# Expert outputs: a table in DRAM that is gathered and added at the end, against accumulating scatters into the residual in DRAM, block by block

## The chip, the cores and the metric

One core of one Trainium2 chip runs the kernel. The metric is the device time of one launch in microseconds (us). TensorE (PE) multiplies and transposes, VectorE (DVE) and ScalarE (ACT) do elementwise work and bring results out of PSUM, GpSimd (POOL) does elementwise work and issues the indirect DMAs, SyncE (SP) issues the weight loads. All DMAs of all queues run on the core's 16 DMA engines.

## The reference

A decoder of two layers over 1024 tokens of width 1024, in float32. Each layer has an attention and pooling half, and then a mixture of experts on which the change acts:

```
x = x + concat(att, pool) @ w_out
h = rms_norm(x)
g = top-1 of 4 groups; (e1, e2) = top-2 of the group's 4 experts        # 16 experts
w1, w2 = softmax over (e1, e2) * p_group                                # the gates
a = silu(h @ w_gate[e]) * (h @ w_up[e]) * gate[e]                        # 256 wide
x = x + sum over e of a[e] @ w_down[e]
```

The output is x after two layers.

## The kernel before

**Stages of a layer.** An input stage (`in_pe`, `in_act`, `in_dve`) turns x into q, k, v, u tile by tile: 8 tiles of 128 tokens, first for q and v, then for k and u, with every product split in three. Attention follows, then the output projection (`out_pe`, `out_act`, `out_dve`), which adds into the residual `xr` (8 tiles, 128 x 1024, in SBUF for the whole kernel), norms it, stores the normed rows in the DRAM tensor `token_rows`, and computes the router's logits. DVE then computes, in one chain of small instructions, where each of the 2048 (token, expert) rows goes: rows are sorted by expert into blocks of 128, at most 31 blocks (`BLOCKS`). Two 16-step matmuls of one-hot matrices (`in_row`, `in_block`) turn the positions into a list of tokens for each block, `row_tok`. How many blocks are used depends on the data; `used` is loaded into a register of each engine. This run uses 22 in the first layer and 23 in the second.

**The expert stage.** In the slot of block t, PE runs `gate_up(t)` (16 matmuls by the profile, line 1521), `xtm(t+1)` (transposes of the next block's rows), `down(t-1)` (8 matmuls, line 1534) and the transposes of `act`. ACT runs the Silu of t, then `moe_down(t-1)`: it copies the upper half of the block's result into `y[slot]`, waits until DVE has copied the lower half, and issues the store of the 512 KB block into the DRAM tensor `y_table` (line 809). Only then it copies `aT(t)`, which PE's `down(t)` reads. `xg` and `y` have three buffers each (`RING`). POOL gathers the rows of block j (`load_rows`, line 578) as soon as the transposes of block j-3 are done. For unused blocks POOL gathers too (all their indices are token 0), while PE, ACT and DVE skip them and only raise their semaphores. SP loads the three weight tensors of an expert, 1 MB each, into four slots as experts end.

**The end of a layer.** When all gathers and stores have been issued and landed, POOL gathers for each tile t and each of its two choices k the rows of `y_table` by `pos_i` (line 594, 16 gathers of 512 KB, four pairs of buffers), and DVE adds them with their gates into `xr` (lines 1261 and 1263), one tile after the other; in the first layer the norms and splits of the next layer's first tiles stand between the additions. ACT's second step of the next input stage waits for `x_ready` of all 8 tiles, and so does SP's load of the third part of `w_in`. After the second layer POOL writes `xr` to `out_x` tile by tile (line 600).

Of the kernel before, what the change touches and what calls it, by code (L numbers as in the profile page):

```python
# [63 lines left out]
C_ALL = C_INV + 16  # L64
# [8 lines left out]
GATHS = 4  # L73
SLOTS = 4
BIAS = BLOCKS


def shape_constants():
# [19 lines left out]
    c[:, C_TOK:C_TOK + 2 * T] = np.tile(P * np.arange(T), 2)[None, :] + row  # L98
# [4 lines left out]
    c[:, C_INV:C_INV + 16] = 1.0 / (1.0 + np.arange(16))  # L103
    return c


def trunk(nc, x, norm1_gain, w_in, q_norm_gain, k_norm_gain, w_pool, pool_scale, w_out,
# [7 lines left out]
    with ctx:  # L115
# [8 lines left out]
        y_table = nc.dram_tensor("y_table", (ROWS, D), f32, kind="Internal").ap()  # L124
# [32 lines left out]
        pos_i = sb("pos_i", [P, 2, T], i32)  # L157
        row_tok = sb("row_tok", [P, 32], i32)
        next_tok = sb("next_tok", [P, RING], i32)
# [10 lines left out]
        u_flat = big[:, AT_U:AT_U + K * 512]  # L170
        raw_in = [W[:, 1, :, :], W[:, 3, :, :], kT_r.rearrange("p (k n) -> p k n", k=K),
# [17 lines left out]
        gath = [big[:, AT_K + 2 * D * i:AT_K + 2 * D * (i + 1)].rearrange("p (k n) -> p k n", k=2) for i in range(GATHS)]  # L189
# [29 lines left out]
        in_block = A[:, 5120:5376].bitcast(f16).rearrange("p (c b) -> p c b", b=32)  # L219
        junk2 = A[:, 6144:6656].bitcast(bf16)  # L220
# [69 lines left out]
        routed = sem("routed")  # L290
        w_loaded = sem("w_loaded")
# [17 lines left out]


# [5 lines left out]
        s_wpool, s_fill = sem("s_wpool"), sem("s_fill")  # L316
# [3 lines left out]
        s_y = [sem(f"s_y{i}") for i in range(RING)]  # L320
        s_gath = [sem(f"s_gath{i}") for i in range(GATHS)]
        s_out = sem("s_out")
# [62 lines left out]
        for name, n in (("lg", T * NR), ("ge", T * EG), ("ee", T * EG), ("gm", T), ("gs", T), ("pt", T),  # L385
                        ("is1", T * 4), ("sm", T), ("goh", T * EG), ("es", T * EPG), ("m1", T), ("oh1", T * 4),
                        ("es2", T * EPG), ("m2", T), ("oh2", T * 4), ("dm", T), ("e2", T), ("rd", T),
                        ("te", NE), ("start", NE), ("cnt", NE), ("posf", 2 * T), ("blk", 2 * T), ("bef", 32), ("M", T * NE)):
# [21 lines left out]
        def _(sp):  # L410
# [16 lines left out]
            with sp.Fori(0, DEPTH) as l:  # L427
# [8 lines left out]
                    .then_inc(s_wpool, 16)  # L436
                sp.wait_ge(rows_t, 1)
# [47 lines left out]
        def _(pool):  # L485
# [24 lines left out]
            for j in range(2 * SEQ // P, BLOCKS):  # L510
                pool.dma_start(y_table[j * P:(j + 1) * P, :], xr[:, 0, :]).then_inc(s_fill, 16)
            with pool.Fori(0, DEPTH) as l:
# [58 lines left out]
                def load_rows(j, slot, m):  # L571
                    if not first(j):
# [4 lines left out]
                    ch.link(nc.gpsimd.tensor_copy(next_tok[:, slot:slot + 1], row_tok[:, ds(j, 1)]))  # L577
                    pool.indirect_dma_start(
                        out=xg[slot], out_offset=None, in_=token_rows,
                        in_offset=bass.IndirectOffsetOnAxis(ap=next_tok[:, slot:slot + 1], axis=0)).then_inc(s_xg[slot], 16)  # L580

                ch.restart()
                steps(pool, BLOCKS, load_rows, ch, ring=RING)


                for i in range(RING):
                    pool.wait_ge(s_y[i], (l + 1) * (16 * USES[i]) + 1)
                    pool.sem_inc(s_passed, 1)
                for t in range(T):
                    if t >= GATHS:  # L590
                        pool.wait_ge(x_ready, upto(l + 1, T, t - GATHS + 1))
                        pool.sem_inc(s_passed, 1)
                    for k in range(2):
                        pool.indirect_dma_start(
                            out=gath[t % GATHS][:, k, :], out_offset=None,
                            in_=y_table, in_offset=bass.IndirectOffsetOnAxis(ap=pos_i[:, k, t:t + 1], axis=0),
                        ).then_inc(s_gath[t % GATHS], 16)
            for t in range(T):
                pool.wait_ge(x_ready, upto(DEPTH, T, t + 1))
                pool.dma_start(out[0, t * P:(t + 1) * P, :], xr[:, t, :]).then_inc(s_out, 16)  # L600
            pool.wait_ge(s_out, 16 * T)


        @block.scalar
        def _(a_):
# [4 lines left out]
            for s in s_y + s_tok:  # L610
                a_.sem_inc(s, 1)
# [37 lines left out]
            with a_.Fori(0, DEPTH) as l:  # L649
# [28 lines left out]
                def in_act(t, par_, h):  # L678
# [917 lines left out]
```

## Time and profile before

| | us |
|---|---|
| median of 3 runs (lowest, highest) | 1797.02 (1796.76, 1799.8) |
| profiled execution, its own time | 1796.23 |
| span of its trace | 1794.2 |
| PE busy in the span | 1496.5 |
| DVE, ACT, POOL busy | 831.2, 485.1, 272.3 |

The span is what the profiler's records cover; the profiled execution took 2.03 us more than it. Busy time of PE includes matmuls that stand in its pipeline. Places in the trace: the expert stage of the first layer lies at 580 to 852 us, that of the second at 1455 to 1740 us.

### The profile page before, as it was taken

What the parts mean: (1) busy time and instruction counts of PE and PEld (TensorE: products, weight loads), DVE (VectorE), ACT (ScalarE), POOL (GpSimd) and SP (SyncE); (2) the same over time, 40 slices, a digit from 0 to 9 for tenths busy, and PEclk for the clock granted to TensorE, in tenths of its full rate; (3) what the DMA queues carried; (4) which work ended last, traced back from release to release, by engine and by line L of the source; (5) the groups of instructions that cost most, each with busy time, mean ns of one, the idle gap of its engine ahead of it and who ended that gap; (6) DMA issues with size and microseconds to landing.
All of it is one profiled execution on the core that took longest, in us unless ns stands there. A gap on an engine that the chain in (4) does not pass through costs nothing.

```text
span 1794.2 us, 23296 instructions
## 1 busy us (share of the span) xinstructions
PE 1496.5 (83%) x6931; PEld 1073.7 (60%) x6932; DVE 831.2 (46%) x2101; ACT 485.1 (27%) x916; POOL 272.3 (15%) x259
## 2 busy tenths in 40 slices
PE   3999977888993999998269998888899749999960
PEld 2887866777882444444158786777768624444430
DVE  3777666565436122211377766665543442222114
ACT  3222156663211011111212212566611201111000
POOL 1200058002001011110300001920200021111114
PEclk8999989999996999999589999899999869999985
DMA  8400020000047588942640002000000845888637
GB/s 302 164 29 0 0 95 1 0 0 0 36 147 263 163 294 299 368 158 88 245 161 0 1 0 94 1 0 0 0 12 35 295 138 172 296 301 293 225 123 287
DMA packets 118473, 228.11 MB, mean 127 GB/s; under 512 B 6184, under 2 KB 72816, under 8 KB 118416
## 3 DMA queue, kind: packets, MB, share of 16 engines
q1 hardware_dynamic: 90352, 129.55, 21.1%
q0 software_dynamic: 18128, 65.71, 10.3%
q10 hardware_dynamic: 9936, 32.14, 4.4%
q8 instruction: 30, 0.49, 0.1%
q14 instruction: 27, 0.22, 0.0%
HBM read 183.33 MB, written 44.04 MB: 127 GB/s over the span
## 4 chain that ended last, share of the span: by engine, by line
PE 71%; DVE 10%; issue 8%; ACT 5%; DMA 4%; ACTq 1%; POOL 0%; DVEq 0%; PEld 0%; POOLq 0%; SPq 0%; PEldq 0%
PE ps L1521 18%; PE ps L1315 17%; PE ps L1448 9%; PE ps L1295 9%; PE ps L1534 8%; PE ps L1408 5%; ACT arena L730 2%; PE ps L1462 2%; DMA arena<-token_rows,next_tok 1%; ACT arena L742 1%; DMA big<-y_table,pos_i 1%; DVE arena L1021 1%; DVE w_in_lo L913 1%; PE ps L1375 1%; PE ps L1377 1%
## 5 line engine op out<-in xcount | busy, mean ns | idle before, releaser
L1295 PE MATMUL ps<-cst,arena 128*128 128x128 f32 x1682 | 247.7, 283 | 145.4 <-DVE arena L884 56.9
L1521 PE MATMUL ps<-big,arena 128*128 x720 | 325.3, 605 | 10.6 <-issue 9.9
L1295 PEld LDWEIGHTS ps<-cst,arena 128*128 128x128 f32 x1682 | 199.1, 145 | 223.2 <-DVE arena L884 59.1
L874 DVE TENSOR_TENSOR arena<-ps,par 128x512 f32<-128x512 f32 x126 | 81.2, 687 | 365.2 <-PE ps L1295 365.2
L1521 PEld LDWEIGHTS ps<-big,arena 128*128 128x128 f32 x720 | 135.5, 193 | 171.5 <-issue 171.5
L1315 PE MATMUL ps<-w_in_hi,hT_hi 128*128 128x512 f32 x512 | 206.8, 404 | 12.6 <-DVE w_in_lo L913 8.6
L1315 PE MATMUL ps<-w_in_lo,hT_hi 128*128 128x512 f32 x512 | 202.2, 395 | 0.0
L1315 PE MATMUL ps<-w_in_hi,hT_lo 128*128 128x512 f32 x512 | 202.2, 395 | 0.0
L1534 PE MATMUL ps<-big,arena 128*128 x360 | 166.6, 607 | 7.0 <-issue 7.0
L1408 PE MATMUL ps<-big,arena 128*128 x1152 | 149.6, 276 | 0.0
L1408 PEld LDWEIGHTS ps<-big,arena 128*128 128x128 f32 x1152 | 144.7, 193 | 5.4
L577 POOL COPY next_tok<-row_tok 128x1 int32 (+1 forms) x62 | 14.9, 240 | 781.7 <-PE ps L1295 450.7
L1021 DVE CUSTOM_DVE_ANT_0 arena<-ps,cst 128x128 f32<-128x128 f32 (+7 forms) x128 | 96.7, 756 | 69.4 <-PE ps L1377 68.4
L730 ACT ACTIVATE arena<-arena,st 128x128 f32<-128x128 f32 (+7 forms) x128 | 99.2, 775 | 79.0 <-DVE st L1021 76.9
L1315 PEld LDWEIGHTS ps<-w_in_hi,hT_hi 128*128 128x128 f32 x512 | 98.3, 192 | 35.3 <-DVE w_in_lo L913 10.4
L1534 PEld LDWEIGHTS ps<-big,arena 128*128 128x128 f32 x360 | 66.6, 195 | 74.8 <-issue 74.8
L1315 PEld LDWEIGHTS ps<-w_in_hi,hT_lo 128*128 128x128 f32 x512 | 97.9, 191 | 21.3
L1315 PEld LDWEIGHTS ps<-w_in_lo,hT_hi 128*128 128x128 f32 x512 | 98.3, 192 | 19.5
L1448 PE MATMUL ps<-w_o_hi,cat_hi 128*128 128x512 f32 x256 | 103.4, 404 | 7.3 <-DVE cat_lo L1081 7.3
L1448 PE MATMUL ps<-w_o_hi,cat_lo 128*128 128x512 f32 x256 | 100.8, 394 | 0.0
L1448 PE MATMUL ps<-w_o_lo,cat_hi 128*128 128x512 f32 x256 | 100.8, 394 | 0.0
L1375 PE MATMUL ps<-k_high,q_parts 128*128 128x512 f32 (+1 forms) x192 | 82.1, 429 | 11.8 <-DVE k_low L996 11.8
(159 smaller groups left out, 1764.4 us busy)
## 6 DMA issues: line engine op xcount, KB each, us to landing
big<-in_w_gate SPq DMA_DIRECT2D x32, 1024.0 KB, 8.5
big<-in_w_up SPq DMA_DIRECT2D x32, 1024.0 KB, 11.2
big<-in_w_down SPq DMA_DIRECT2D x32, 1024.0 KB, 13.0
y_table<-arena ACTq DMA_DIRECT2D x45, 512.0 KB, 7.0
big<-in_w_in SPq DMA_DIRECT2D x18, 1024.0 KB, 10.6
big<-in_w_out SPq DMA_DIRECT2D x4, 2048.0 KB, 10.2
token_rows<-arena ACTq DMA_DIRECT2D x16, 512.0 KB, 2.8
y_table<-x_res POOLq DMA_DIRECT2D x15, 512.0 KB, 9.5
```

The costliest lines, as they stand in the source:

```text
L730: sc.activation(pr[b][:, 0:nk], pr[b][:, 0:nk], ACT.Exp, scale=-1.0, bias=st[:, 64 + n:65 + n], accum_out=st[:, 80 + n:81 + n]).then_inc(p ...
L742: sc.activation(prT[b][:, 0:nb, :], ps[:, 4, 0:nb * P] .rearrange("p (a c) -> p a c", c=P), ACT.Copy).then_inc(pt0_ev, 1)
L874: ins = ve.tensor_tensor(out=dst[:, 4 * h:4 * h + 4, :], in0=ps[:, banks + h, :].rearrange("p (a c) -> p a c", c=P), in1=spread(gain[:, 4 ...
L1021: ve.tensor_tensor_reduce(out=pr[b][:, 0:nk], in0=ps[:, 2 * b:2 * b + 2, :].rearrange("p a c -> p (a c)")[:, 0:nk], in1=cst[:, C_MASK + SE ...
L1295: ins = te.transpose(ps[:, bank + i // 4, (i % 4) * P:(i % 4 + 1) * P], src, ident)
L1315: ins = te.matmul(ps[:, 2 + 2 * par_ + i, :], a[par_][:, k, :], b[:, k, :], start=k == 0 and n == 0, stop=k == K - 1 and n == 2)
L1375: te.matmul(ps[:, 2 * b + c // 512, 0:w], q_parts[a][:, i * P:(i + 1) * P], k_high[a][:, c:c + w], start=True, stop=False)
L1408: ins = te.matmul(ps[:, 6 + b, 0:P], prT[b][:, j, :], v[:, j, ds(p * P, P)], start=j == 0, stop=j == i)
L1448: ins = te.matmul(ps[:, 2 * par_ + h, :], a[par_][:, k, :], b[:, k, :], start=k == 0 and n == 0, stop=k == K - 1 and n == 2)
L1462: ins = te.matmul(ps[:, 6 + par_, 0:P], h2T[par_][:, k, :], wr_all[:, ds(l * (K * NR) + k * NR, P)], start=k == 0, stop=k == K - 1)
L1521: ins = te.matmul(ps[:, 2, :], xgT[:, k, :], big[:, ds(at + k * 2 * FE, 2 * FE)], start=k == 0, stop=k == K - 1)
L1534: ins = te.matmul(ps[:, 4 + h, :], aT[:, k, :], big[:, ds(at + (E_GU + k * D + 512 * h), 512)], start=k == 0, stop=k == 1)
```

## The change

The kernel's output tensor becomes the residual in DRAM for the expert stage, with 31 x 128 spare rows behind its 1024. In the output projection ACT writes each tile of `xr` to it. The gates are not applied at the end but in the activation: for each block a column of 128 gates (`list_gate`) is made, by cutting the 32 bits of a gate into three integers (11, 11 and 10 bits), sending them through 16 more matmuls of the one-hot matrices, and putting them together. `y[slot]` is then added to the rows `row_dst` of the output by a scatter with `compute_op=add`, issued by POOL. Entries of a block that hold no row, and the whole of unused blocks, go to spare rows. Two scatters may name the same token, so ACT raises `y_whole` for block t only when the scatters of all blocks before t have landed (`s_add`); unused blocks don't wait for that. All 31 scatters are issued in each layer. At the start of the second layer SP waits for all 31 scatters of the first and reads the 8 tiles of `xr` back; after the second layer POOL waits for the last scatter, and the first 1024 rows are the result. `y_table`, its 15 filling stores at the start, `pos_i`, `next_tok`, the 32 gathers and the 32 additions at the layers' ends, and the 8 final stores are gone.

```diff
+C_SPARE = C_INV + 16          # SEQ + 1 + 128*block + row: the spare row of each entry
+AHEAD = 5
+OUT_ROWS = SEQ + ROWS
 # SP, at the start of layer l
+                with sp.If(l > 0):
+                    sp.wait_ge(s_add, upto_added(l, 0))
+                    for t in range(T):
+                        sp.dma_start(xr[:, t, :], out[t * P:(t + 1) * P, :]).then_inc(s_again[t], 16)
+                    for t in range(T):
+                        sp.wait_ge(s_again[t], l * 16)
+                        sp.sem_inc(x_ready, 1)
 # POOL
-            for j in range(2 * SEQ // P, BLOCKS):
-                pool.dma_start(y_table[j * P:(j + 1) * P, :], xr[:, 0, :]).then_inc(s_fill, 16)
-                    ch.link(nc.gpsimd.tensor_copy(next_tok[:, slot:slot + 1], row_tok[:, ds(j, 1)]))
-                steps(pool, BLOCKS, load_rows, ch, ring=RING)
-                for t in range(T):
-                    if t >= GATHS:
-                        pool.wait_ge(x_ready, upto(l + 1, T, t - GATHS + 1))
-                    for k in range(2):
-                        pool.indirect_dma_start(
-                            out=gath[t % GATHS][:, k, :], out_offset=None,
-                            in_=y_table, in_offset=bass.IndirectOffsetOnAxis(ap=pos_i[:, k, t:t + 1], axis=0),
-                        ).then_inc(s_gath[t % GATHS], 16)
-            for t in range(T):
-                pool.wait_ge(x_ready, upto(DEPTH, T, t + 1))
-                pool.dma_start(out[0, t * P:(t + 1) * P, :], xr[:, t, :]).then_inc(s_out, 16)
+                def add_rows(j):
+                    pool.wait_ge(y_whole, upto(l, BLOCKS, j + 1))
+                    pool.indirect_dma_start(
+                        out=out, out_offset=bass.IndirectOffsetOnAxis(ap=row_dst[:, j:j + 1], axis=0),
+                        in_=y[j % RING], in_offset=None, compute_op=ALU.add).then_inc(s_add, 16)
+                for j in range(BLOCKS):
+                    load_rows(j, j % RING, j // RING)
+                    if j == 0:
+                        pool.wait_ge(s_base, (l + 1) * (16 * T))
+                    if j >= AHEAD:
+                        add_rows(j - AHEAD)
+                for j in range(BLOCKS - AHEAD, BLOCKS):
+                    add_rows(j)
+            pool.wait_ge(s_add, upto_added(DEPTH, 0))
 # ACT
-                        if h == 0:
-                            a_.wait_ge(x_ready, upto(l, T, T))
                     a_.dma_start(token_rows[ds(t * P, P), :], xs2[par_]).then_inc(s_tok[par_], 16)
+                    a_.dma_start(out[ds(t * P, P), :], xr[:, t, :]).then_inc(s_base, 16)
@@ moe_down
-                    a_.wait_ge(s_y[slot], l * (16 * USES[slot]) + 16 * m + 1)
+                    a_.wait_ge(y_whole, upto(l, BLOCKS, t + 2 - RING))
                     sc.activation(y[slot][:, 512:1024], ps[:, 5, :], ACT.Copy).then_inc(y1_ready, 1)
                     a_.wait_ge(y0_ready, upto(l, BLOCKS, t + 1))
                     a_.wait_ge(y1_ready, upto(l, BLOCKS, t + 1))
-                    a_.dma_start(y_table[ds(t * P, P), :], y[slot]).then_inc(s_y[slot], 16)
+                    if not first(t):
+                        a_.wait_ge(s_add, upto_added(l, t))
+                    a_.sem_inc(y_whole, 1)
 # DVE, after block_e: dve.wait_ge(s_base, ...), three bit cuts, a cast, a compare, three
 # products into in_gate, three small ones for row_dst; after rows_evac(0) three more that
 # put list_gate together; in_low(l + 1, 0) moves behind them
-                ch.link(ve.tensor_copy(pos_i[:, :, :].rearrange("p k t -> p (k t)"), R("posf")))
-                    ve.tensor_tensor(out=act, in0=ps[:, 2, FE:2 * FE], in1=sg, op=ALU.mult).then_inc(a_ready, 1)
+                    ve.scalar_tensor_tensor(out=act, in0=ps[:, 2, FE:2 * FE], scalar=list_gate[:, ds(t, 1)], in1=sg,
+                                            op0=ALU.mult, op1=ALU.mult).then_inc(a_ready, 1)
-                for t in range(T):
-                    dve.wait_ge(s_gath[b], l * (16 * 2 * (T // GATHS)) + 32 * (t // GATHS + 1))
-                    ch.link(ve.scalar_tensor_tensor(out=xr[:, t, :], in0=gath[b][:, 0, :], scalar=gate_w[:, 0, t:t + 1],
-                                                    in1=xr[:, t, :], op0=ALU.mult, op1=ALU.add))
-                    ve.scalar_tensor_tensor(out=xr[:, t, :], in0=gath[b][:, 1, :], scalar=gate_w[:, 1, t:t + 1],
-                                                in1=xr[:, t, :], op0=ALU.mult, op1=ALU.add).then_inc(x_ready, 1)
 # PE, after xtm(0)
+                pe.wait_ge(gate_parts, upto(l, 1, 1))
+                for c in range(2 * T):
+                    ins = te.matmul(ps[:, 7, 0:96], in_row[:, c, :], in_gate[:, c, :, :].rearrange("p k b -> p (k b)"),
+                                    start=c == 0, stop=c == 2 * T - 1)
```

On POOL, the end of the block loop and of the layer, before. `arena<-token_rows` is a gather of a block's rows, `big<-y_table` a gather for the final additions; the names in brackets are semaphores that are waited for.

```order
L577 COPY next_tok<-row_tok 128x1 [waits s_xg0]
L578 DMA arena<-token_rows,next_tok 128x1024 [waits s_pool]
L587 ISA
L587 ISA [waits s_y0]
L594 DMA big<-y_table,pos_i 128x1024 [waits s_y1,s_y2]
L594 DMA big<-y_table,pos_i 128x1024 x7
L591 ISA
L594 DMA big<-y_table,pos_i 128x1024 [waits x_ready]
```

The same place after the change, where `out_x<-arena,x_res` is a scatter that adds:

```order
L594 DMA arena<-token_rows,row_tok 128x1024 [waits xtm_done,s_xg2]
L602 DMA out_x<-arena,x_res 4992x1024 [waits y_whole]
L590 REGISTER_ALU
L591 REGISTER_ALU [waits xtm_done]
L594 DMA arena<-token_rows,row_tok 128x1024 [waits s_xg0]
L602 DMA out_x<-arena,x_res 4992x1024 [waits y_whole] x3
L600 REGISTER_ALU
L602 DMA out_x<-arena,x_res 4992x1024 [waits y_whole]
```

The scatter of block j-5 stands behind the gather of block j, and the last five stand at the end, where the 16 gathers stood.

On ACT, one slot of the expert stage, before (`L813` is the Silu, `L806` the copy of a block's upper half, `L817` the copy of `aT`):

```order
L812 ISA
L813 ACTIVATE arena<-ps 128x256 [waits gu_done]
L805 ISA [waits dn_done]
L806 ACTIVATE arena<-ps 128x512 [waits s_y1]
L809 ISA [waits y1_ready,y0_ready]
L809 DMA y_table<-arena 128x1024
L817 ACTIVATE arena<-ps 128x256 [waits a_t_done]
```

and after the change:

```order
L827 ISA
L828 ACTIVATE arena<-ps 128x256 [waits gu_done]
L818 ISA [waits dn_done]
L819 ACTIVATE arena<-ps 128x512 [waits y_whole]
L823 ISA [waits y1_ready,y0_ready]
L832 ACTIVATE arena<-ps 128x256 [waits s_add,a_t_done]
```

The store has left ACT's queue, and the wait for the scatters before this block stands in its place, ahead of the copy of `aT`.

## Rows read from the trace of the kernel before

**Rows 1.** The page, part 1: busy time and share of the span.

```profile
PE 1496.5 (83%) x6931; PEld 1073.7 (60%) x6932; DVE 831.2 (46%) x2101; ACT 485.1 (27%) x916; POOL 272.3 (15%) x259
```

**Rows 2.** Windows: stretch, length, each engine's busy us, clock, DMA share, GB/s.

```profile
609.00:768.00 159.00, 158.88 (x474) 77.19 (x473) 30.75 (x53) 19.13 (x42) 15.18 (x27) 1.00 0.88 310
```

**Rows 3.** Timeline: start, length, engine, line; first layer's expert stage on POOL.

```profile
607.60 0.18 POOL L577 COPY next_tok<-row_tok 128x1 int32 x1 [11.35 <-PE ps L1295]
...
839.55 0.18 POOL L577 COPY next_tok<-row_tok 128x1 int32 x1 [10.07 <-PE ps L1295]
```

**Rows 4.** Issue to landing of the block gathers, line 578, 590 to 843 us.

```profile
DMA to landing us min/median/max: 4.3/6.0/7.2
```

**Rows 5.** Issue to landing of the table stores, line 809, 590 to 843 us.

```profile
L809 ACTq DMA_DIRECT2D y_table<-arena x20: 337/339/356, 611.8 to 831.9; - x20
DMA to landing us min/median/max: 2.6/7.2/8.9
```

**Rows 6.** Timeline: one slot, and the next slot's down matmuls.

```profile
612.25 0.38 ACT L817 ACTIVATE arena<-ps 128x256 f32<-128x256 f32 x1 [0.71 <-DVE arena L1220]
...
618.55 3.60 PE L1534 MATMUL ps<-big,arena 128*128 x8
```

**Rows 7.** Timeline and chain of waits: the end of the first layer.

```profile
852.58 0.18 POOL L577 COPY next_tok<-row_tok 128x1 int32 x1 [11.39 <-PEq L1572]
...
866.21 0.97 POOL L578 DMA_INDIRECT arena<-token_rows,next_tok  x1 [0.50 <-POOL next_tok L577]
867.48 0.94 POOL L594 DMA_INDIRECT big<-y_table,pos_i  x1 [0.30 <-issue]
...
877.64 1.06 ACT L624 ACTIVATE arena<-x_res 128x1024 f32<-128x1024 f32 x1 [16.53 <-DVE x_res L1263]
881.18 1.97 PE L1295 MATMUL ps<-cst,arena 128*128 128x128 f32 x8 [29.46 <-DVE arena L884]
```

**Rows 8.** Timeline, last row chain of waits: PE in the second layer's first tiles.

```profile
886.81 0.79 PE L1315 MATMUL ps<-w_in_hi,hT_hi 128*128 128x512 f32 x1 [3.66 <-DVE hT_lo L902]
...
894.49 0.39 PE L1315 MATMUL ps<-w_in_hi,hT_lo 128*128 128x512 f32 x1
...
926.19 1.97 PE L1295 MATMUL ps<-cst,arena 128*128 128x128 f32 x8 [8.39 <-DVE arena L884]
...
928.16 11.54 PE ps L1315 x48
```

**Rows 9.** DMA, 843 to 881 us in 40 slices of 0.95 us, and issues.

```profile
GB/s 203 181 375 0 0 0 0 0 0 0 47 229 358 285 280 399 412 410 423 392 397 395 338 350 330 187 233 267 129 246 323 354 375 397 397 392 414 418 414 418
big<-in_w_in SPq DMA_DIRECT2D x2, 1024.0 KB, 10.0
```

**Rows 10.** Timeline and windows: the end of the second layer.

```profile
1740.14 0.18 POOL L577 COPY next_tok<-row_tok 128x1 int32 x1 [12.78 <-PEq L1572]
1778.36 0.53 POOL L600 DMA_DIRECT2D out_x<-x_res  x1 [2.93 <-DVE x_res L1263]
1740.00:1785.00 45.00, 0.00 (x0) 0.00 (x0) 20.34 (x17) 0.00 (x0) 24.68 (x32) 0.52 0.91 339
1785.00:1794.20 9.20, 0.00 (x0) 0.00 (x0) 0.00 (x0) 0.00 (x0) 0.00 (x0) 0.50 0.00 0
```

**Rows 11.** Page part 6: the read of one tile of x, alone in its queue.

```profile
x_res<-in_x SPq DMA_DIRECT2D x1, 512.0 KB, 3.5
```

**Rows 12.** Timeline: tables and the first block of the first layer.

```profile
567.67 0.69 DVE L1116 TENSOR_TENSOR arena<-arena,cst 128x512 f32<-128x512 f32 x1
572.27 0.40 PE L1498 MATMUL ps<-arena 128*128 128x32 f16 x8 [10.76 <-DVE arena L1194]
575.78 0.18 DVE L1207 TENSOR_SCALAR block_e<-arena 128x32 int32<-128x32 f32 x1
581.92 1.29 DVE L874 TENSOR_TENSOR arena<-ps,par 128x512 f32<-128x512 f32 x2 [0.30 <-PE ps L1295]
584.46 8.87 PE L1521 MATMUL ps<-big,arena 128*128 x16 [2.57 <-issue]
```

More of the change, by code:

```diff
@@ L72 @@
 RING = 3
-GATHS = 4
 SLOTS = 4
+AHEAD = 5
+OUT_ROWS = SEQ + ROWS
 BIAS = BLOCKS
@@ L97, in shape_constants @@
     c[:, C_JJ:C_JJ + P] = np.arange(P)
-    c[:, C_TOK:C_TOK + 2 * T] = np.tile(P * np.arange(T), 2)[None, :] + row
+    c[:, C_TOK:C_TOK + 2 * T] = np.tile(P * np.arange(T), 2)[None, :] + row + 1
     c[:, C_DESC:C_DESC + 4] = 4 - np.arange(4)
@@ L103, in shape_constants @@
     c[:, C_INV:C_INV + 16] = 1.0 / (1.0 + np.arange(16))
+    c[:, C_SPARE:C_SPARE + 32] = SEQ + 1 + P * np.minimum(np.arange(32), BLOCKS - 1)[None, :] + row
     return c
@@ L188, in trunk @@
                 for i in range(SLOTS)]
-        gath = [big[:, AT_K + 2 * D * i:AT_K + 2 * D * (i + 1)].rearrange("p (k n) -> p k n", k=2) for i in range(GATHS)]
         def ring(at, size, n=2, inner=None):
@@ L290, in trunk @@
         routed = sem("routed")
+        gate_parts = sem("gate_parts")
+        gates_listed = sem("gates_listed")
+        y_whole = sem("y_whole")
         w_loaded = sem("w_loaded")
@@ L319, in trunk @@
         s_xg = [sem(f"s_xg{i}") for i in range(RING)]
-        s_y = [sem(f"s_y{i}") for i in range(RING)]
-        s_gath = [sem(f"s_gath{i}") for i in range(GATHS)]
-        s_out = sem("s_out")
+        s_base, s_add = sem("s_base"), sem("s_add")
+        s_again = [sem(f"s_again{t}") for t in range(T)]
         s_ms = sem("s_ms")
@@ L607, in _ @@
             for s in (params, q_high_in, k_high_in, win_top, gain_in, sd1, sqz_done, sdz, cat_top, v_copied, u_copied, t_evac, p_ready, pt0_ev, at_ev, sd2,
-                      ge_exp, dm_exp, silu_done, aT_ready, y1_ready):
+                      ge_exp, dm_exp, silu_done, aT_ready, y1_ready, y_whole):
                 a_.sem_inc(s, BIAS)
-            for s in s_y + s_tok:
+            for s in s_tok:
                 a_.sem_inc(s, 1)
@@ L825, in maybe_down @@
                         a_.sem_inc(y1_ready, 1)
-                        a_.sem_inc(s_y[slot], 16)
+                        a_.sem_inc(y_whole, 1)
                 def maybe_act(t, slot, m):
@@ L1197, in _ @@
                 dve.wait_ge(listed, upto(l, 1, 1))
-                ve.tensor_copy(row_tok[:, :], ps[:, 2, 0:32]).then_inc(rows_known, 1)
+                ve.tensor_scalar(row_tok[:, :], ps[:, 2, 0:32], -1.0, 0.0, ALU.add, ALU.max).then_inc(rows_known, 1)
                 ch.link(ve.tensor_copy(start_i[:, 0:NE], R("start")))
@@ L1209, in _ @@
                 dve.sem_inc(s_passed, 1)
+                dve.wait_ge(s_base, (l + 1) * (16 * T))
+                dve.sem_inc(s_passed, 1)
+                bits = gate_w[:, :, :].rearrange("p k t -> p (k t)").bitcast(i32)
+                ve.tensor_scalar(gate_bits[:, 0, :], bits, 0x7FF, None, ALU.bitwise_and)
+                ve.tensor_scalar(gate_bits[:, 1, :], bits, 11, 0x7FF, ALU.logical_shift_right, ALU.bitwise_and)
+                ch.link(ve.tensor_scalar(gate_bits[:, 2, :], bits, 22, None, ALU.logical_shift_right))
+                ch.link(ve.tensor_copy(R("parts"), gate_bits[:, :, :].rearrange("p k c -> p (k c)")))
+                parts = R("parts").rearrange("p (k c) -> p k c", k=3)
+                tt(R("tmp3", 32), spread(R("blk"), 32), count, ALU.is_equal)
+                for k in range(3):
+                    ins = ve.tensor_tensor(out=in_gate[:, :, k, :], in0=R("tmp3", 32), in1=spread(parts[:, k, :], 32),
+                                           op=ALU.mult)
+                ins.then_inc(gate_parts, 1)
+                ch.link(ve.tensor_scalar(R("spare"), ps[:, 2, 0:32], 0.0, None, ALU.is_equal))
+                tt(R("spare"), R("spare"), cst[:, C_SPARE:C_SPARE + 32], ALU.mult)
+                ch.link(ve.scalar_tensor_tensor(out=row_dst[:, :], in0=ps[:, 2, 0:32], scalar=-1.0, in1=R("spare"),
+                                                op0=ALU.add, op1=ALU.add))
                 used = dve.value_load(start_i[0:1, NE:NE + 1], min_val=2 * SEQ // P, max_val=BLOCKS)
```

69 lines of the change are left out of this document (35 added, 34 removed).

## The prediction

> **What bounds the kernel now.** I read the page first: PE is busy for 83% of the span, every other engine for less than half [rows 1]. So a change that takes nothing from PE can only win where PE stands. The windows show no such place inside the expert stage: in 159 us PE is busy for 158.88 at full clock, while the DMA engines are already at 0.88 [rows 2]. A slot there lasts (839.55 - 607.60) / 20 = 11.6 us, 20 slots lying between these two rows [rows 3]. The places are the ends of the two layers. In the first, PE ends its last block at about 852 and starts again at 881.18, idle for 29.46 us [rows 7]; after that it works with holes until 926.19, where it falls into an even pace [rows 8]. In the second, PE has ended when POOL is let go at 1740.14, and the last bytes land at about 1785, since the DMA share is 0.91 until then and 0 after; the 9.2 us behind it have no DMA and stay [rows 10]. The rows thus offer at most 45 us at the end, and some 50 between the layers.
>
> **What an adding scatter costs.** The trace has none. Unit of the sum: 512 KB at about 400 GB/s, which the slices with full DMA engines show (392 to 423), is 1.3 us of all 16 engines, one pass [rows 9]. A scatter reads y, reads the destination and writes it. Lower bound: one pass (1.3), if the second read is free; nothing can be below that, the bytes are the store's. Upper bound: three passes (3.9), each transfer after the other. I take two, 2.6 us, the middle, because a plain copy also reads and writes in one pass and the addition has one read more.
>
> The Trainium skill, Collectives: The Full Stack, "The bandwidth ceiling: the fold count and why AG ≠ RS ≠ AR", says that the addition itself is free and its second source read costs, with 62.28 against 32.35 GB/s measured. By that the scatter is 2.5 us and the sum below moves by 2 us; no row here can show it.
>
> **The expert stage.** Removed per slot: ACT's issue of the store (0.34 us [rows 5]), which nobody waits for. DVE's product with the gate has the same 256 elements. Added: a chain from block to block. `y_whole(t)` releases the scatter of t on POOL, the scatter must land, and only then ACT raises `y_whole(t+1)`. POOL's gather of block t+5 stands before that scatter, but it is released in the middle of the slot, before y is whole, and is no later than now. Landing from issue: lower bound 4.3, the fastest gather [rows 4]; upper bound 13.2, median gather plus median store, 6.0 + 7.2 [rows 4, 5]. I take the store's 7.2, the nearest row, plus the extra pass counted twice (1.3 x 2), since the weights use the other half of the engines: 9.8. With some 0.9 us for POOL's start and ACT's step the chain is 10.7 us, below the 11.6 of a slot: nothing added. The cover is thin. Behind the waiting ACT stands the copy of `aT`, at 612.25 now, needed by the down matmuls at 618.55 [rows 6]: a single late scatter of up to 6 us is absorbed. DMA work rises by one pass per slot, from 0.88 x 11.6 = 10.2 to 11.5 us [rows 2]. That is full, but the weights are loaded three experts ahead, so PE should not wait.
>
> The Trainium skill, DMA: Bandwidth & Descriptors, "Anatomy of one DMA", gives 2.0 us plus bytes over 436 GB/s. By it the scatter would land in some 4.4 us and the chain would never matter. The trace disagrees for stores beside weights (7.2 against 3.2), so the row counts [rows 5].
>
> **Between the layers.** Used blocks are 0 to 21. Gather 25 and scatter 20 go out in the last full slot. From 852.3 on the engines have: `w_in` and `wpool`, 2.36 MB, 5.9 us; gathers 26 to 30, 5 x 1.3 = 6.5; scatters 21 to 30, 10 x 2.6 = 26, nine of which add nothing to any token but are issued. Issue on POOL, about 15 x 1.24 us = 19 [rows 7], is hidden by that. Sum 38.4, plus 1.3 for the last to land: 892.0. SP then reads x back: the first tile takes 3.5 us [rows 11] and 0.4 for issue and semaphore, so `x_ready` of tile 0 comes at 895.9, where it was 877.64 [rows 7]: 18.3 later. Back comes what the interleaved additions cost. From x of tile 0 to PE's even pace were 926.19 - 877.64 = 48.6 us [rows 8]. Without them: 9.2 to the first product and 8.1 for it, unchanged (to 894.9), then PE only: transposes 1.3, two products of 24 matmuls at 11.54 / 2 = 5.8 [rows 8], 0.6 for the turn of q, in all 30.8. DVE's work in that time (the split of w_in, 4.5, two norms and the q norm) fits beside it. Gain 17.8. Net +0.5 (18.3 - 17.8).
>
> **The end.** From 1740.1: four gathers 5.2, scatters 22 to 30, 9 x 2.6 = 23.4, landing 1.3: 1770.0 instead of 1785 [rows 10]. Gain 15.
>
> **Small terms.** Per layer: the cast of pos_i goes, a small instruction like that of block_e (-0.2) [rows 12]; ACT's issue of the last base store but one stands before the last tile's square (+0.4, from 0.34 and its wait) [rows 5]. DVE's new table work, 7 instructions of about 0.2, 4 of 0.7 and a register load of some 1.2, runs from 576.0 to about 581.5, and the first evacuation began at 581.92 [rows 12]: hidden; the split of w_in (4.5) moves behind it, where DVE waits anyway. PE's 16 new matmuls have three times the columns of those at 0.40 for 8, so 1 to 1.6 us, in the 2.57 us of issue before 584.46, and the first gather starts 0.9 earlier without POOL's copy [rows 12]: 0 to +1, taken +0.3. Together +0.5, twice +1. At the start 15 stores of 512 KB go, while PE had its operands: nothing.
>
> **Sum.** +0.5 - 15 + 1 = -13.5 on the span of 1794.2, so 1780.7, and 1782.7 with the 2.03 us around it. The profiled execution (1796.23) was 0.8 below the median of the runs, so 1784 (1783.5). Each us more or less per scatter counts 19 times (10 + 9).
>
> **Rivals.**
> 1. The cheap scatter, one pass: 19 x 1.3 = 25 us less, 1759. For: the store wrote the same bytes. Against: the second read must go through the same engines.
> 2. The dear drain, three passes, with the chain still hidden: 19 x 1.3 = 25 more, 1809. The point of no change is 13.5 / 19 = 0.7 above my price, at 3.3 us per scatter. For: 4 KB rows to scattered places. Against: 400 GB/s holds for the gathers of the same rows.
> 3. The chain decides, slower than before: if a scatter takes over 10.7 us from issue to landing beside the weights, the slot follows it. At the upper bound, 13.2 + 0.9 = 14.1, it is 2.5 us for 21 + 22 slots, 107, less 6 us of cover in each layer: 95 more, 1879. At a landing of 11.5 us it is some 22 more, 1806. For: DMA share 0.88 and a cover of 0.9 us. Against: once the last expert is loaded the queues empty, and lag is made up there.
> 4. The DMA engines are overfull and PE waits for weights: at three passes 0.88 x 11.6 + 2.6 = 12.8 us of work per slot, 1.2 too much for 14 slots in each layer, 34 at most, of which the three experts ahead (some 35 us) cover all. It gives nothing by itself.
>
> **How the numbers follow.** Forecast (1.9 to 3.3 us per scatter, chain hidden): 0.50, with its own range 1770 to 1797. Rival 1: 0.17. Rival 2: 0.13. Rival 3: 0.18. Rival 4 or anything else: 0.02. A measurement of this kernel tells about 0.2% (3.6 us) from no change. Faster by more: rival 1 and nearly all of the forecast, 0.64. Within: the seam between forecast and rival 2, 0.08. Slower: rivals 2 and 3, 0.28. Range 1760 to 1830: half of the cheap case and the worse half of the chain's stay outside.
>
> **What would show it.** In the profile after: the scatters' issue to landing, about 10 us while weights load, and ACT's copy of `aT` still less than 2 us behind the y copy; if it is 5 us or more behind, rival 3 acts. The slot stays 11.6 us. The first reads of x from out begin at about 892 and PE's next transposes at about 899; PE then reaches its even pace some 27 us later. After the last down matmuls 30 us pass until the last DMA. The forecast is wrong if a scatter occupies the engines for under 1.9 or over 3.3 us in those two drains, if reading x back is not done at the speed of a plain load, or if the gates' table moves the first block by over 1 us.

## The result and the profile after

| | before | after |
|---|---|---|
| median of 4 runs each | 1797.99 us | 1778.43 us (1776.35 to 1780.45) |
| ratio | | 0.989, interval 0.9873 to 0.9907 |
| profiled execution, its span | 1796.23, 1794.2 | 1777.19, 1775.4 |

The forecast was 1784, its own range 1770 to 1797. Measured again beside two experiments (see 6), the same kernel had the ratio 0.9933 (0.9915 to 0.995), median 1783.44. So the change is worth 0.7 to 1.1%, 12 to 20 us; below, the 18.8 us between the two profiled spans are laid out.

First the page (part 1), then two windows: the steady expert stage, and the drain at the end where nothing but adding scatters is in the queues. Columns of the windows as in [rows 2].

```profile
PE 1489.7 (84%) x6963; PEld 1073.2 (60%) x6964; DVE 801.0 (45%) x2095; ACT 485.4 (27%) x916; POOL 308.4 (17%) x204
```
```profile
613.00:772.00 159.00, 158.57 (x472) 76.98 (x471) 31.54 (x53) 19.13 (x42) 34.86 (x27) 1.00 0.99 310
...
1756.00:1769.00 13.00, 0.00 (x0) 0.00 (x0) 0.00 (x0) 0.00 (x0) 3.85 (x3) 0.50 1.05 211
```

Against [rows 1], DVE has lost 30 us (the 32 additions of 1.28 us, 41 in all, less 11 of new table work), and POOL has 36 more: a scatter takes it 1.58 us to issue, a gather 0.98. Against [rows 2], PE's busy time is the same, 158.6 of 159, while the DMA share rose from 0.88 to 0.99: in this stretch every slot is full of transfers and PE does not notice. The second window gives the price of a scatter: 524,288 bytes at 211 GB/s are 2.48 us of all 16 engines.

POOL (line 602 the scatter, 594 the gather) and ACT (819 the copy of y, 832 the copy of `aT`) in one slot, and the landings of the scatters between 590 and 840 us:

```profile
837.03 1.57 POOL L602 DMA_INDIRECT out_x<-arena,x_res  x1 [3.40 <-ACTq L824]
...
848.81 1.58 POOL L602 DMA_INDIRECT out_x<-arena,x_res  x1 [3.40 <-ACTq L824]
```
```profile
847.08 0.60 ACT L819 ACTIVATE arena<-ps 128x512 f32<-128x512 f32 x1 [4.01 <-PE ps L1560]
848.04 0.38 ACT L832 ACTIVATE arena<-ps 128x256 f32<-128x256 f32 x1 [0.36 <-DVE arena L1251]
```
```profile
L602 POOL DMA_INDIRECT out_x<-arena,x_res x20: 1572/1576/1622, 616.5 to 837.0; - x20
DMA to landing us min/median/max: 5.8/8.8/10.5
```

The slot is unchanged: 19 slots from 616.5 to 837.0 are 11.6 us each, as in [rows 3].

A scatter issued at 837.03 lands, by the median, at 845.8, and the next is issued at 848.81. So ACT finds `s_add` raised: `aT` follows y's copy after 0.36 us. Of the 11.8 us between two scatters 8.8 are the landing; less those 0.4 for ACT's step the cover of the chain (what it could grow by before it sets the length of the slot) is some 2.6 us. POOL's own start is not in this; with the 0.9 us that the prediction took for ACT's step and POOL's start together it is 2.1, where the prediction had 0.9.

The chain of waits between the layers (start, length, what):

```profile
880.28 15.54 DMA out_x<-arena,x_res
895.84 0.37 SPq L452
...
899.78 1.16 ACT arena L638 x2
...
903.32 1.98 PE ps L1321 x8
...
908.95 7.55 PE ps L1341 x24
...
930.94 1.09 PE ps L1321 x8
```

The last scatter is issued at 880.28 behind a queue that needs 15.5 us more; x is read at 895.84, and PE's even pace begins at 930.94, where it was 926.19 [rows 8].

The end:

```profile
1739.00:1768.00 29.00, 0.00 (x0) 0.00 (x0) 0.00 (x0) 0.00 (x0) 17.80 (x13) 0.56 0.98 217
1768.00:1771.00 3.00, 0.00 (x0) 0.00 (x0) 0.00 (x0) 0.00 (x0) 0.00 (x0) 0.50 0.93 184
1771.00:1775.40 4.40, 0.00 (x0) 0.00 (x0) 0.00 (x0) 0.00 (x0) 0.00 (x0) 0.50 0.03 6
```

Full engines until 1771, then 4.4 us; in [rows 10] full until 1785, then 9.2.

**Where the 18.8 us come from.** At the end of the first layer's last down matmuls the kernel is 1.8 us later (853.53 against 851.72), at the even pace 4.75, at the last product of the second layer's input stage 3.3, at its last down matmuls 1.9 earlier. From there to the end of the span: 38.2 instead of 55.1 us, 16.9 less. So the gain lies in the end; what the middle adds and gives back nearly cancels. The 16.9 are three things: from POOL's release to the last bytes 12.6 less (1740.14 to 1785 before, 1738.69 to 1771 now), the tail without transfers 4.8 less (4.4 for 9.2), and the release 0.5 later behind the last matmul.

The last down matmuls of the two layers, before, and of the second layer after (those of the first stand in 6):

```profile
846.33 5.39 PE L1534 MATMUL ps<-big,arena 128*128 x8 [3.52 <-issue]
...
1732.60 6.51 PE L1534 MATMUL ps<-big,arena 128*128 x8 [3.52 <-issue]
```
```profile
1733.48 3.70 PE L1560 MATMUL ps<-big,arena 128*128 x8 [2.75 <-issue]
```

### The profile page after: what moved, and what is told of

It reads as the page before. It is cut to its first block, busy times and chain, and to the rows that moved or that the text cites. A ratio compares the mean times of both kernels' runs of the same rounds, so it can differ in the third digit from the quotient of the medians.

```text
span 1775.4 us, 23244 instructions
## 1 busy us (share of the span) xinstructions
PE 1489.7 (84%) x6963; PEld 1073.2 (60%) x6964; DVE 801.0 (45%) x2095; ACT 485.4 (27%) x916; POOL 308.4 (17%) x204
## 4 chain that ended last, share of the span: by engine, by line
PE 72%; DVE 8%; issue 7%; ACT 5%; DMA 4%; ACTq 1%; POOL 1%; SPq 0%; PEldq 0%; DVEq 0%; POOLq 0%; PEld 0%
PE ps L1547 18%; PE ps L1341 17%; PE ps L1321 10%; PE ps L1474 9%; PE ps L1560 8%; PE ps L1434 5%; ACT arena L742 2%; PE ps L1488 2%; ACT arena L754 1%; DMA out_x<-arena,x_res 1%; DMA arena<-token_rows,row_tok 1%; DVE arena L1036 1%; PE ps L1401 1%; PE ps L1403 1%; DVE arena L1130 1%
## 5 line engine op out<-in xcount | busy, mean ns | idle before, releaser
L1547 PE MATMUL ps<-big,arena 128*128 x720 | 322.5, 601 | 9.2 <-issue 8.1
L1560 PE MATMUL ps<-big,arena 128*128 x360 | 162.1, 593 | 5.4 <-issue 5.4
L594 POOL DMA_INDIRECT arena<-token_rows,row_tok x62 | 60.6, 978 | 600.2 <-issue 307.2
L1434 PE MATMUL ps<-big,arena 128*128 x1152 | 150.4, 277 | 0.0
L602 POOL DMA_INDIRECT out_x<-arena,x_res x62 | 98.0, 1580 | 154.9 <-ACTq L824 140.8
L1341 PEld LDWEIGHTS ps<-w_in_lo,hT_hi 128*128 128x128 f32 x512 | 97.5, 191 | 19.3
## 6 DMA issues: line engine op xcount, KB each, us to landing
big<-in_w_down SPq DMA_DIRECT2D x32, 1024.0 KB, 15.5
big<-in_w_in SPq DMA_DIRECT2D x18, 1024.0 KB, 10.8
```

The costliest lines, as they stand in the source:

```text
L594: pool.indirect_dma_start(out=xg[slot], out_offset=None, in_=token_rows, in_offset=bass.IndirectOffsetOnAxis(ap=row_tok[:, j:j + 1], axis= ...
L602: pool.indirect_dma_start(out=out, out_offset=bass.IndirectOffsetOnAxis(ap=row_dst[:, j:j + 1], axis=0), in_=y[j % RING], in_offset=None, ...
L1341: ins = te.matmul(ps[:, 2 + 2 * par_ + i, :], a[par_][:, k, :], b[:, k, :], start=k == 0 and n == 0, stop=k == K - 1 and n == 2)
L1434: ins = te.matmul(ps[:, 6 + b, 0:P], prT[b][:, j, :], v[:, j, ds(p * P, P)], start=j == 0, stop=j == i)
L1547: ins = te.matmul(ps[:, 2, :], xgT[:, k, :], big[:, ds(at + k * 2 * FE, 2 * FE)], start=k == 0, stop=k == K - 1)
L1560: ins = te.matmul(ps[:, 4 + h, :], aT[:, k, :], big[:, ds(at + (E_GU + k * D + 512 * h), 512)], start=k == 0, stop=k == 1)
```

## The experiments

**1. Is it the addition that costs?** Blocks 22 to 30 written without adding. In layer 2 block 22 is a used one, so of its rows too the sum is left out.

```diff
-  in_=y[j % RING], in_offset=None, compute_op=ALU.add)
+  in_=y[j % RING], in_offset=None, **({"compute_op": ALU.add} if j < 22 else {}))
```

> The changed kernel, but the scatters of blocks 22 to 30, which add only to spare rows behind the output, write without adding (9 in each layer). Theory A (the second read through the DMA engines is what an adding scatter costs; 2.46 us now, some 1.3 for a plain one): 18 x 1.16 = 21 us less than the changed kernel's 1778, or 18 less if POOL's issue (1.88 us each) sets the pace of the drain instead: 1757 to 1760. Rival B (4 KB rows at scattered places, or POOL's issue, set the pace, and the addition costs nothing): 1775 to 1779. In the profile: the drains move 350 to 400 GB/s under A, 210 under B.

Measured: 0.9809 (0.9792 to 0.9826) of the kernel before, 1761.49 us, 1.5 over theory A's range; span 1759.8, 15.6 less than the changed kernel's. The drains, first between the layers, then at the end:

```profile
874.00:883.00 9.00, 0.00 (x0) 0.00 (x0) 0.00 (x0) 0.00 (x0) 3.79 (x4) 0.50 1.02 415
```
```profile
1746.00:1754.00 8.00, 0.00 (x0) 0.00 (x0) 0.00 (x0) 0.00 (x0) 3.32 (x4) 0.50 1.00 406
```

The same rows to the same places move at 406 to 415 GB/s when they are written, 211 when added: 1.28 against 2.48 us, a factor of 1.9. POOL's issue falls too, from 1.56 to 0.96 us. x is read at 885.07, 10.8 us sooner. Rival B falls. The drains gave what theory A said: 11.3 us between the layers (29.6 from POOL's release to the read of x, where it was 40.9) and 10.9 from the last down matmuls to the end of the span, 22 together. That the span is only 15.6 shorter comes mostly from two kinds of place where PE ran at a lower granted clock here. The last down matmuls of both layers took 5.39 us and 3.70 in the changed kernel's trace, 3.4 together. From the second layer's first expert product to its first down matmul 23.3 us passed, and 19.3 in the changed kernel's trace; the windows here and there:

```profile
1452.80:1476.10 23.30, 20.27 (x50) 9.52 (x51) 5.75 (x5) 1.15 (x3) 0.94 (x1) 0.83 0.14 46
```
```profile
1463.12:1482.40 19.28, 16.26 (x50) 8.04 (x51) 5.76 (x5) 1.15 (x3) 0.94 (x1) 1.00 0.17 54
```

See 6 for what this clock belongs to.

**2. What do the surplus transfers cost?** POOL loads `used` and issues nothing for unused blocks but a 64-byte DMA each.

```diff
+  with pool.If(used > j):
+      scatter()
+  with pool.Else():
+      pool.dma_start(out[SEQ + j * P:SEQ + j * P + 1, 0:16], y[j % RING][0:1, 0:16]).then_inc(s_add, 16)
```

> The changed kernel, but POOL loads the number of used blocks (22) and issues neither gathers beyond block 22 nor scatters beyond block 21; a 64-byte DMA stands for each in its semaphore. Theory A (the two drains of scatters are what holds PE between the layers and the end): the last scatter of layer 1 lands at about 866 instead of 895.8, the last of layer 2 at about 1746 instead of 1770.7; 30 + 25 less, 1724 (1718 to 1735). Rival B (between the layers something else is nearly as late, the halves of w_in or the work on them): only the end moves, 25 less, 1753.

Measured: 0.9733 (0.9714 to 0.9753), 1750.17 us, outside the 1718 to 1735 and near rival B's number, but rival B is not the reason: x was read 19.5 us sooner, which it excluded. POOL and SP between the layers:

```profile
857.88 1.58 POOL L612 DMA_INDIRECT out_x<-arena,x_res  x1 [0.30 <-issue]
...
872.61 0.49 POOL L622 DMA_DIRECT2D out_x<-arena  x1 [0.28 <-issue]
```
```profile
866.00:880.00 14.00, 0.00 (x0) 0.00 (x0) 0.00 (x0) 0.00 (x0) 3.41 (x7) 0.50 0.27 74
```

After the last real scatter POOL issues its stand-ins one by one, waiting for earlier ones, until 872.6, with the DMA engines at 0.27; x is read at 876.4. The transfers were gone, but their issues and waits held the place. Hence the next version, in which nothing stands for a left-out scatter: waits go by counts worked out from `used` (`done` holds the used blocks of the layer before). For the left-out gathers of the first layer 8 DMAs of 64 bytes are still issued behind the last scatter, from 860.33 on for 4.1 us; the read of x does not wait for them.

```diff
-  a_.wait_ge(s_add, upto_added(l, t))
+  a_.wait_ge(s_add, (l * done + t) * 16)
-  sp.wait_ge(s_add, upto_added(l, 0))
+  sp.wait_ge(s_add, used * 16)
```

> The changed kernel without gathers beyond block 22 and without scatters beyond the last used block, and with nothing in their place: the counts that SP, ACT and POOL wait for are worked out from the number of used blocks. (In the first skipping kernel POOL issued 15 small DMAs there, one after the other until 872.6, waited for earlier ones, and x was read at 876.4 while the DMA share was 0.27.) Theory A (the stand-ins held x back, nothing else): the last scatter, issued at 857.9, lands at about 865; x is read at 866 instead of 876 and the end comes some 4 us sooner: 1736 (1732 to 1741). Rival B (the halves of w_in and the work on them are nearly as late): only the end moves, 1744 to 1748.

Measured: 0.9613 (0.9593 to 0.9632), 1730.66 us. SP's row and PE's:

```profile
866.82 4.63 SPq L452 DMA_DIRECT2D x_res<-out_x  x8
```
```profile
876.30 1.96 PE L1347 MATMUL ps<-cst,arena 128*128 128x128 f32 x8 [21.51 <-issue]
```

x is read at 866.82, 29 us sooner than in the changed kernel, as theory A said; the time is 1.3 us under its range. Rival B falls. PE starts 9.5 us after the read and not 7.5. Of that 0.85 stands ahead of the first square (4.79 us after the read, 3.94 before); that w_in's second chunk beside the read is behind it is likely, but not shown.

**3. How thick is the cover of the chain?** Additions on POOL between the wait and the scatter, one in the first kernel, three in the second.

```diff
+  for _ in range(1 if j < 20 else 0):
+      ch.link(nc.gpsimd.tensor_tensor(out=xr[:, 3, :], in0=xr[:, 1, :], in1=xr[:, 2, :], op=ALU.add))
```

> The changed kernel with one addition of 128x1024 on POOL, on rows that nobody reads any more (about 2.1 us, 2.2 with its wait), between the wait for the whole y and the scatter, for blocks 0 to 19 of each layer. Theory A (the chain from scatter to scatter has some 2.6 us of cover, as the changed kernel's trace has it: issue at 837.03, landed at 845.8, next issue at 848.8): nothing in the slots, at most +5 us in all, 1778 to 1783. Rival B (the cover is the 0.9 us of the prediction, or less, the next issue being late for another reason): 1.3 us for 19 slots in each layer, 50 less some 6 per layer absorbed: 1810 to 1830.

> The same with three such additions (about 6.5 us) before each of these scatters. Theory A (a chain longer than the slot sets the slot): 8.8 + 0.9 + 6.5 = 16.2 against 11.6, 4.6 us for 19 slots in each layer, less some 6 us of cover per layer: 160 us more, 1938 (1900 to 1960). Rival B (the chain is off PE's path, because ACT and DVE can run ahead of it by the ring's three buffers): under 15 us more, 1793 at most.

Measured: 0.9943 (0.9926 to 0.9961), 1788.35 us with one, 1.0827 (1.0809 to 1.0845), 1947.11 us with three. ACT in the first, and in the second:

```profile
723.41 0.38 ACT L834 ACTIVATE arena<-ps 128x256 f32<-128x256 f32 x1 [3.94 <-DMA out_x<-arena,x_res]
725.83 0.38 ACT L830 ACTIVATE arena<-ps 128x256 f32<-128x256 f32 x1 [2.04 <-PE ps L1549]
```
```profile
833.85 0.39 ACT L834 ACTIVATE arena<-ps 128x256 f32<-128x256 f32 x1 [6.31 <-DMA out_x<-arena,x_res]
834.13 0.38 ACT L830 ACTIVATE arena<-ps 128x256 f32<-128x256 f32 x1
```

One addition (2.34 us, and 0.28 to the issue) uses the cover up: ACT now waits for the scatter before 16 of the 19 copies of `aT` in the first layer's slots, by 3.9 us on average, and PE loses only 2.3 and 2.4 us in the two stretches of 240 us that make up the slots. The kernel is 2 to 10 us slower than the changed one, by which of its two ratios one takes. Its median is 5 us over theory A's range and 22 under rival B's. Three additions (7.2 us) make the chain the slot: the scatters follow one another in 14 to 18 us, and the kernel is 150 us slower than the one before, where 1938 us had been worked out. Rival B of the second falls: the chain is real. Its cover can be read here more directly: from the issue of a scatter to POOL's next addition most blocks have 9.8 us (692.15 to 701.92) and some have 6.5, against a slot of some 11.7. So the chain is about 2 us away from setting the time, not the 2.6 that the first kernel of this experiment was planned with.

**4. The gates alone,** on the kernel before: table, gathers and additions stay, the additions multiply by 1.

```diff
-  ve.tensor_tensor(out=act, in0=ps[:, 2, FE:2 * FE], in1=sg, op=ALU.mult)
+  ve.scalar_tensor_tensor(out=act, in0=ps[:, 2, FE:2 * FE], scalar=list_gate[:, ds(t, 1)], in1=sg,
+                          op0=ALU.mult, op1=ALU.mult)
```

> The kernel before with one part of the change alone: the gates are listed by block and multiplied into the activation (the final additions multiply by 1 instead); table, gathers and additions at the end stay. Theory A (this part is hidden): 0 to +1 us per layer, 1796 to 1800, last down matmuls still 5 us or more at a clock of about 0.7. Rival B (the shorter last down matmuls, 3.70 us instead of 5.39 and 6.51, and the higher clock in the first blocks come with this part, from its 16 added matmuls or its moved split of w_in): 6 to 9 us less, 1788 to 1792.

Measured: 0.9998 (0.9989 to 1.0008), 1795.77 us. The last down matmuls in the two layers, and the added ones:

```profile
847.93 5.39 PE L1560 MATMUL ps<-big,arena 128*128 x8 [3.52 <-issue]
...
1733.62 6.74 PE L1560 MATMUL ps<-big,arena 128*128 x8 [3.52 <-issue]
```
```profile
584.40 1.49 PE L1567 MATMUL ps<-arena 128*128 128x96 f16 x16
587.15 7.12 PE L1547 MATMUL ps<-big,arena 128*128 x16 [1.26 <-issue]
```

This part is worth nothing, either way. PE's 16 matmuls stand where its 2.57 us of issue stood [rows 12]; 1.26 are left. Rival B falls: the shorter last down matmuls do not come with it. Its DMA share is 0.04 from 1785 and 0 from 1787 with the span ending at 1794.5, so this part of the change does not shorten the tail.

**5. The base store on ACT.** It was moved to POOL, and in a version on top of the skipping one behind ACT's square.

```diff
-  a_.dma_start(out[ds(t * P, P), :], xr[:, t, :]).then_inc(s_base, 16)
+  pool.wait_ge(x_upd, upto(l, T, t + 1))
+  pool.dma_start(out[t * P:(t + 1) * P, :], xr[:, t, :]).then_inc(s_base, 16)
```

> The changed kernel, but the 8 stores of the residual into the output in each layer are issued by POOL as soon as its tile is updated, not by ACT ahead of the next tile's square. Theory A (those issues on ACT, 0.34 us each and 1.22 us for one of the last, make the end of the output projection 2.7 us later and the router 4 us later in each layer): 4 to 8 us less than 1778: 1770 to 1774. Rival B (the lateness comes from the transfers' share of the DMA engines or from somewhere else): 1777 to 1780, and the first expert product of layer 1 stays 3.6 us later than in the kernel before.

> The same with one more edit: ACT issues the store of the residual tile after that tile's square and square root, not ahead of the next tile's. Theory A (the issue on ACT delays the last tile's path to the router by the 1.25 us that the kernel with these stores on POOL gave back, once per layer): 2.5 us less than the kernel it stands on. Rival B (the granted clock at the start of the output projection, 0.59 or 1.00 in the first 7 us, worth up to 2.7 us in each layer, moves more than this edit does): anything from 3 us more to 5 us less, and only the stretch from the last residual addition to the router's last transposes shows the 1.25 us.

Measured: 0.9924 (0.991 to 0.9938), 1781.26 us; and 0.9604 (0.9589 to 0.9619), 1725.58 us. In the changed kernel ACT's issues read:

```profile
545.67 0.42 ACTq L781 DMA_DIRECT2D token_rows<-arena  x1
546.13 1.22 ACTq L782 DMA_DIRECT2D out_x<-x_res  x1
547.40 1.06 ACT L801 ACTIVATE arena<-x_res 128x1024 bf16<-128x1024 f32 x1 [12.66 <-issue]
```

From the last residual addition to the normed tile are 5.81 us there (544.35 to 550.16), 4.56 with the store on POOL, 4.56 with it behind the square, 4.57 in the kernel before. So the edit gives its 1.25 us in its place, and neither time shows it: the first kernel's ratio lies between the changed kernel's two, the second's interval overlaps that of the kernel that it stands on. Theory A of the first falls; rival B's time was missed by 1.3 us, and the first expert product is 2.1 us later than in the kernel before (586.56 against 584.46), not 3.6. The second gained 5.1 us by the medians where theory A had 2.5 and rival B up to 5, with intervals that overlap, so its time decides nothing. Only the stretch above shows the 1.25. The other 2.7 us by which the changed kernel leaves the projection later are there at its first tile, before any store. The windows of the first 7 us of its matmuls, before, after, and the changed kernel once more:

```profile
436.00:443.00 7.00, 6.87 (x30) 5.70 (x31) 1.10 (x2) 0.00 (x0) 0.00 (x0) 1.00 0.01 2
```
```profile
436.33:443.33 7.00, 7.00 (x20) 5.52 (x21) 0.96 (x2) 0.00 (x0) 0.00 (x0) 0.61 0.01 2
```
```profile
436.73:443.73 7.00, 7.00 (x24) 5.65 (x25) 0.97 (x2) 0.00 (x0) 0.00 (x0) 0.76 0.01 2
```

Of the change only the 15 filling stores at the start lie ahead of this place, and they are gone from the second and third window alike. Yet the granted clock is 1.00, 0.61 and 0.76, and 30, 20 and 24 matmuls start in the same 7 us. (1.00 is TensorE's higher level, 2.4 GHz, and 0.50 the lower, 1.2 GHz; a mean between them is a stretch with both.)

**6. Is the clock at these edges the kernel's own?** The changed kernel again, and with one and three memsets of POOL before x is declared ready at the start.

```diff
+  for _ in range(1):
+      ch.link(nc.gpsimd.memset(xr[:, 7, :], 0.0))
   pool.sem_inc(x_ready, 1)
```

> The changed kernel unchanged, beside the two that follow: 1778 within 3 us. Its granted clock in the first 7 us of the output projection of layer 1 (436 to 443) was 0.59, in the kernel before 1.00; if that belongs to the kernel, it is 0.59 again.

> The changed kernel with one memset of 128x1024 on POOL (0.5 to 1.1 us) before x is declared ready at the very start, so that all that follows is late by that much or by nothing. Theory A (the granted clock at the edges of stages, which decides 2 to 4 us at the start of the output projection and at the last down matmuls, turns with shifts of a microsecond): the time moves by something other than the shift, up to 4 us either way, and the last down matmuls or the first products of the projection change between 1.00 and 0.5 to 0.7. Rival B (the clock at these places belongs to the code around them): the time rises by the shift, 0 to 1.1 us, and the clocks there stay.

> The same with three memsets (1.5 to 3.3 us). Theory A: up to 5 us either way beside the shift, with other clocks at these places. Rival B: 1.5 to 3.3 us more, the same clocks.

Measured: 1783.44 us (1776.05 to 1789.37), where 1778 within 3 was expected, 1785.65 and 1782.78; ratios 0.9933, 0.9932, 0.9921 with intervals of about 0.0015 either way. The last down matmuls of the first layer, in the changed kernel, then in the same kernel again:

```profile
849.83 3.70 PE L1560 MATMUL ps<-big,arena 128*128 x8 [2.65 <-issue]
```
```profile
845.97 5.39 PE L1560 MATMUL ps<-big,arena 128*128 x8 [2.64 <-issue]
```

One kernel has 3.70 us in one execution and 5.39 in another, and the shifted ones 3.70 and 5.16, 5.39 and 3.69 in the two layers. The first matmuls of the projection came 1.7 and 2.0 us later than in the run without memsets; the three intervals of the ratios overlap, so the times say nothing about the shift. Rival B falls by the first pair of rows: the clock at these edges is not a property of the code alone, since it differs between two profiled executions of one kernel. Theory A is not shown. Both shifted executions have 23.1 and 22.7 us from the second layer's first expert product to its first down matmul, where the two without a shift have 19.3 and 19.5, but whether the shift does that can't be told from these four. Nor is the execution told apart from the chip, since the sets of runs were taken on several. The clock moves a span by a few us, and differences of that size between two kernels mean nothing until their rows are read.

**7. Reading x first.** On top of the last version of 5, SP issues two tiles of x, then w_in's second chunk and w_pool, then the other six, and only then reports the tiles one after the other.

```diff
+  for t in range(2):
+      sp.dma_start(xr[:, t, :], out[t * P:(t + 1) * P, :]).then_inc(s_again[t], 16)
   load_in(l, 1, 2)
```

> The skipping kernel with the later base store, and one more edit: between the layers SP reads the first two tiles of x back before it issues the second chunk of w_in (2 MB) and w_pool, which stood ahead of the read and so beside the last two scatters. Theory A (the engines were shared with that chunk while the last scatter landed, 9.7 us instead of the 5.8 that one takes alone): the scatter lands 3 to 4 us sooner and tile 0 is there 1 to 2 us sooner after it: 5 us less than the kernel it stands on, 1720 (1717 to 1723). Rival B (the chunk is needed as early as tile 0, since ACT splits it right after the first square, at 869.6): the second product waits for it, and the gain is 0 to 2 us, 1723 to 1727.

Measured: 0.9623 (0.9611 to 0.9636), 1729.79 us, no gain. SP's queue and ACT's first square:

```profile
861.13 3.20 SPq L447 DMA_DIRECT2D x_res<-out_x  x2
864.70 0.99 SPq L435 DMA_DIRECT2D big<-in_w_in  x2
865.96 0.85 SPq L451 DMA_DIRECT2D wpool<-in_w_pool  x1
866.95 7.55 SPq L455 DMA_DIRECT2D x_res<-out_x  x6
```
```profile
874.66 1.06 ACT L665 ACTIVATE arena<-x_res 128x1024 f32<-128x1024 f32 x1 [12.38 <-SPq L458]
```

The scatter landed sooner as expected, 6.0 us after its issue (855.13 to 861.13) and not 9.7. But the report of tile 0 stands behind all issues of SP, and six of them take 7.55 us in a full queue: ACT hears of tile 0 at 874.66, 13.5 us after SP's first read, where the kernel without this edit needed 5.6. Neither theory had this. The order with the report of tile 0 ahead of the last six was not run.

The best version is that of 5, without surplus transfers and with the later base store: 0.9604 of the kernel before, 3% under the changed kernel.

## Why the prediction held, step by step

- **The scatter's price:** right. 2.48 us against 2.6 taken. Rivals 1 and 2 (1.3 and 3.9) fall with it. The Trainium skill, Collectives: The Full Stack, "The bandwidth ceiling: the fold count and why AG ≠ RS ≠ AR", has 62.28 against 32.35 GB/s for a collective, a ratio of 1.93, and puts it down to the second source read. The trace agrees with the ratio: the drains give 406 against 211 GB/s, 1.92.
- **The slot:** right that nothing is added. The landing was 8.8 instead of 9.8 us and the cover some 2 us instead of 0.9; rival 3 was real but further off than its 0.18 and its 1806 made it: its mechanism appears with one added POOL operation. The DMA share came to 0.99, as the 11.5 us of work in 11.6 said, and PE did not wait for weights.
- **Between the layers:** right in its parts. Square of tile 0 after the read 3.94 us (3.9 taken), then to the even pace 31.2 (30.8). x came 3.8 later than forecast, of which 2.6 is POOL's later release (854.95, and 852.3 in the sum), and 1.2 a longer drain (40.9 against 39.7). Net of the 1.8 that it came in with, the pace is 3.0 later, +0.5 taken.
- **The end:** mis-sized on both sides. From POOL's release to the last bytes 32.3 us, 29.9 taken. The tail "stays" was wrong: 4.4 instead of 9.2. The long tail goes with kernels whose last DMAs are plain stores issued by POOL: experiment 4 has 9, and the first kernel of experiment 2, which ends in 64-byte stores, 8 from its last bytes at 1739.5 to 1747.4. Those that end in scatters have some 3.5 to 6, with or without addition (the changed kernel, experiment 1, the later ones of 2 and 5). Why is open.
- **Small terms:** the base store cost 1.25 us per layer, not 0.4, since one issue of 1.22 us stands ahead of a square; the gates' table cost nothing where 0.3 per layer were taken.
- **Not in the working at all:** the granted clock. The start of the projection took 2.7 us from the gain, the last down matmuls gave 1.7 and 2.8 to it (5.39 and 6.51 to 3.70), and the first blocks of the second layer 2.9. By experiment 6 that is in large part the execution's, not the change's. That the forecast of 1784 lies 0.6 and 5.6 us above the two medians, 1783.4 and 1778.4, is therefore good to a few us and no better.
- **Luck:** the mechanism held, but the closeness of the number is in part chance. Three terms came out worse than in the sum: between the layers by 2.5 us, the drain at the end by 2.4, the base stores of both layers by 1.7. Against them stand two things that the sum did not have, the shorter tail (4.8) and the clock (4.7 net, in this pair of traces).

## What to carry to other kernels

In this kernel an accumulating scatter costs the DMA engines 1.9 times a plain one. It costs no time where PE has other work and its landing stays within the slot, and it counts in full where PE, or the end of the kernel, waits for a drain. So count what is issued in the drain: here 17 of the 62 scatters moved nothing that anybody reads, and leaving them and their gathers out gave some 50 us, more than twice the change itself. And a transfer that is left out is only gone when its issue, its semaphore step and the waits of the next ones are gone too.

## What the runs showed that was not expected

- POOL's issue of an indirect DMA with addition takes 1.56 to 1.59 us, without 0.96 to 0.98, and the difference goes with the addition alone (experiment 1).
- An issue is not a constant of SP either: reading x back took 0.47 us per tile in the changed kernel (8 in 3.78), 1.26 where six followed w_in into a busy queue, and 1.6 for two behind the last scatter (experiment 7).
- The median of one kernel moved by 5 us between two sets of runs, while the kernel before stayed within 2.2 us (1795.85 to 1797.99) in four.
